# Projecting the second heads' forget gate and queries ahead of the second output gate in layer 1

## The reference

```python
h = rmsnorm(x, pre_norm[layer])
proj = h @ w_in[layer]
(hq, hf, hi, hz, nq, kc, vc, ks, vs, kw, vw, ng, nz) = split(proj)
o_h = hgrn2_mixer(heads(hq), heads(hf), heads(hi), lower_bounds[layer])
o_h = rmsnorm(o_h, hgrn_out_norm[layer]) * silu(hz)
o_n = nsa_mixer(heads(nq), kc, vc, ks, vs, kw, vw, ng, ...) * silu(nz)
x = x + rmsnorm(concatenate([o_h, o_n]) @ w_out[layer], post_norm[layer])
```

## Time and profile before

| | before |
|---|---|
| median of 3 runs | 2059.6 us (2058.7 to 2061.26) |
| profiled execution, its own time | 2056.29 us |
| its span, first to last instruction | 2054.5 us |
| busy TensorE / VectorE / ScalarE / POOL | 2022.3 / 1406.0 / 1061.5 / 105.8 us |
| mean granted clock of TensorE | 0.996 of 2.4 GHz |
| chain that ended last | TensorE 79%, VectorE 4%, ScalarE 2% of the span |

### The profile page before, as it was taken

One profiled execution on the slowest core, in us unless ns is written; L12 is line 12 of the kernel. 1 busy time (PEld: TensorE's weight loads), 2 busy tenths in 40 slices (PEclk: granted clock), 3 DMA queues, 4 the chain that ended last, 5 costly groups with the idle time before them and its releaser, 6 DMA issues.

```text
span 2054.5 us, 30481 instructions
## 1 busy us (share of the span) xinstructions
PE 2022.3 (98%) x12911; PEld 1726.1 (84%) x12911; DVE 1406.0 (68%) x1813; ACT 1061.5 (52%) x1557; POOL 105.8 (5%) x121
## 2 busy tenths in 40 slices
PE   8999999998899999999999999999999999999998
PEld 7889779887778888888898888888888888988887
DVE  6777867778877767647865765766676567656655
ACT  6555646456545544546354545555445554544543
POOL 0100111000210100000000000000100000000000
PEclk9999999999999999999999999999999999999999
DMA  7653345643346754455454465655544554554652
GB/s 268 181 189 124 114 168 173 207 145 103 109 159 221 242 192 147 158 170 164 170 199 164 164 205 188 211 193 196 203 165 144 166 182 165 185 185 144 198 197 87
DMA packets 191090, 356.67 MB, mean 174 GB/s; under 512 B 6317, under 2 KB 83305, under 8 KB 190954
## 3 DMA queue, kind: packets, MB, share of 16 engines
q1 hardware_dynamic: 188218, 344.76, 50.6%
q0 software_dynamic: 2736, 9.96, 1.3%
HBM read 353.65 MB, written 1.05 MB: 173 GB/s over the span
## 4 chain that ended last, share of the span: by engine, by line
PE 79%; DVE 4%; ACT 2%; issue 1%; POOL 0%; DVEq 0%; ACTq 0%
PE bank L2146 15%; PE bank L2150 15%; PE bank L2156 15%; PE bank L2188 13%; PE bank L2192 7%; PE bank L2201 2%; PE bank L2170 2%; PE bank L2173 2%; PE bank L2176 1%; DVE raw_r L2714 1%; PE bank L2222 1%; PE bank L2463 1%; PE bank L2230 1%; PE bank L2241 1%; PE bank L2411 1%
## 5 line engine op out<-in xcount | busy, mean ns | idle before, releaser
L2714 DVE TENSOR_TENSOR raw_r<-raw,high 128x2048 fp32r<-128x2048 f32 (+2 forms) x299 | 674.3, 2266 | 85.4 <-ACT high L2490 84.2
L2490 ACT ACTIVATE high<-raw 128x2048 fp32r<-128x2048 f32 (+2 forms) x299 | 564.6, 1896 | 207.7 <-PE bank L2156 174.7
L2146 PE MATMUL bank<-high,units_r 128*128 128x512 f32 (+3 forms) x1504 | 592.0, 395 | 2.6 <-ACT high L2490 2.1
L2150 PE MATMUL bank<-high,units_r 128*128 128x512 f32 (+2 forms) x1472 | 567.3, 387 | 0.5 <-DVE units_r L2735 0.4
L2156 PE MATMUL bank<-raw_r,units_r 128*128 128x512 f32 (+3 forms) x1504 | 397.0, 385 | 0.0
L2146 PEld LDWEIGHTS bank<-high,units_r 128*128 128x128 f32 x1504 | 283.9, 189 | 62.1 <-issue 4.7
L2156 PEld LDWEIGHTS bank<-raw_r,units_r 128*128 128x128 f32 x1504 | 279.7, 188 | 57.0 <-DVE raw_r L2714 0.3
L2150 PEld LDWEIGHTS bank<-high,units_r 128*128 128x128 f32 x1472 | 278.1, 189 | 54.1 <-DVE units_r L2735 1.7
L2188 PE MATMUL bank<-units_r,high 128*128 128x512 f32 x1152 | 288.2, 392 | 0.0
L2188 PEld LDWEIGHTS bank<-units_r,high 128*128 128x128 f32 x1152 | 208.4, 189 | 38.1
L2192 PEld LDWEIGHTS bank<-units_r,raw_r 128*128 128x128 f32 x1152 | 157.2, 190 | 11.2
(11 more groups left out here) (383 smaller groups left out, 2198.7 us busy)
## 6 DMA issues: line engine op xcount, KB each, us to landing
raw<-in_ffn_w_dram SPq DMA_DIRECT2D x132, 1024.0 KB, 5.1
raw<-in_w_in_dram SPq DMA_DIRECT2D x104, 1024.0 KB, 5.1
raw<-in_w_out_dram SPq DMA_DIRECT2D x24, 1024.0 KB, 5.0
raw<-in_cross_wkv_dram SPq DMA_DIRECT2D x16, 1024.0 KB, 5.0
raw<-in_w_branch_dram SPq DMA_DIRECT2D x12, 1024.0 KB, 4.9
raw<-in_cross_wq_dram SPq DMA_DIRECT2D x8, 1024.0 KB, 5.1
raw<-in_cross_wo_dram SPq DMA_DIRECT2D x8, 1024.0 KB, 4.9
raw<-in_w_in_dram SPq DMA_DIRECT2D x4, 832.0 KB, 4.5
```

Source lines behind the costliest of these rows:

```text
L2146: pe.matmul(o, h.high(k0 + k)[:, span], p.hi[k][:, cols], start=start and k == 0, stop=False, skip_group_check=True)
L2150: pe.matmul(o, h.low(k0 + k)[:, span], p.hi[k][:, cols], start=False, stop=False, skip_group_check=True)
L2490: done = act.activation(high, raw, ACT.Copy)
L2714: done = dve.tensor_tensor(low, raw, high.bitcast(F32), ALU.subtract)
```

## The change

```diff
@@ -1453,8 +1453,11 @@
             yield from nz_proj(0)
             yield from hgrn_v(0)
             yield from hgrn_z(0)
+            if l:
+                yield from hgrn_qf(1)
             yield from nz_proj(1)
-            yield from hgrn_qf(1)
+            if l == 0:
+                yield from hgrn_qf(1)
             yield from hgrn_v(1)
             yield from hgrn_z(1)
             plan.give_pairs(h, ("prod", f"{N}.hz1", 1))
```

## The result

| | before | after |
|---|---|---|
| median | 2057.31 us (9 runs, 2055.87 to 2061.26) | 2063.68 us (9 runs, 2063.12 to 2068.15) |
| ratio, 95% interval | | 1.0033 [1.0023, 1.0043] |
| profiled execution / span | 2056.29 / 2054.5 us | 2063.49 / 2061.7 us |
| TensorE idle, 440 to 600 us | 12.1 us | 15.3 us |
| TensorE work lost to the lower clock, there | 3.8 us | 8.1 us |

The change makes the kernel slower by 0.33%, or 6.4 us between the medians.

The account below looks back on a forecast made before the run. TensorE's work plus its waits bound the kernel. New waits of 14.9 plus 3.8 of clock, 18.7 us, against 15.3 removed give +3.4 us: profiled execution 2059.7, median 2063.0 us, range 2056.5 to 2069.5.

Parts of the forecast that it names:

- What bounds the kernel: TensorE, busy 98% of the span; reordering layer 1's second-half projections can change only waits and clock, winning at most 15.3 us.
- The softplus block: ScalarE runs softplus right behind the split, until 473.25 us; TensorE's pv_few then waits 0.9 us for the small keys' copy.
- The first gate: TensorE's first turn_four of s010 waits 5.0 us for VectorE's gates, ready at 482.8 us; one clock fall follows.
- Rival 2: Faster: first gate held only by exponentials, wait 1.6 us, no fall; -1.9, or -6.5 with level 2 on time; chance 0.12.
- 'same': Second heads' step directly behind s010's second-branch turns: TensorE waits 2.5 us for the key's exponential on ScalarE.
- The second gate: Gate of s110: VectorE finishes 15.2 us after the joint scores start, TensorE arrives after 13.5, so it waits 1.7 us.
- Levels 4 and 2: Second heads' late levels, too little TensorE work between: waits of 1.1, 0.1, 2.9 and 0.7, together 4.8 us.
- The clock: Two falls of TensorE's granted clock, behind the first gate and at levels 4 and 2, 1.9 us each, 3.8 in all.
- Rival 1: Slower beyond measurement: third clock fall at 'same', or VectorE 1 us later at the first gate; +5.3 to +6.3; chance 0.41.
- the bound of 0.2%: Two executions can't be told apart within about 0.2%, 4.1 us; chances: faster 0.10, same 0.49, slower 0.41.

Follow-up runs that it names:

- e2: The changed kernel with the second heads' recurrence of layer 1 begun three units of projection work later, so the 'same' step comes later: 2058.68 us, ratio 1.0006.
- e3: The changed kernel with only the forget gate projected ahead of the second output gate and the queries left behind it: 2054.49 us, ratio 0.9985 to before.
- e11: e3 with softplus left in place but VectorE's forget, bounded and decay begun five projection steps later: 2057.22 us, ratio 0.9996 to before.
- e10: The changed kernel with 3 extra matmuls on TensorE, only ahead of the few keys' step (pv_few of s010): 2063.85 us, ratio 1.0030 to before.
- e5: The changed kernel with extra matmuls on TensorE sized to its six waits, 14.6 us in all: 2059.54 us, ratio 1.0009 to before.
- e6: e3 with all arithmetic on the forget gate (softplus, forget, bounded, decay) begun six projection steps later: 2063.35 us, ratio 1.0023 to before.

## Why the prediction was right or wrong

- *What bounds the kernel* held. Instruction counts are the same, and nearly the whole difference lies in one stretch: the last turn behind it (hT10) starts 7.2 us later and the span is 7.2 longer, with 6.7 of it from the stretch and 0.5 from ahead of it.
- *The softplus block, 0.9.* Right: it runs from 463.97 to 473.86 us and the few keys wait 0.90. But "the waits of 1.0 and 1.1 us were followed by full clock" did not carry over: behind this wait of 0.9 the clock fell, in the change and in e2, e3 and e11 alike. That fall cost nothing, as e10 shows.
- *The first gate, 5.0, held by VectorE.* Right: 5.01 once nothing falls ahead of it (e10), 3.64 as it stood. e11 confirms the mechanism and its size against the exponentials alone: 1.5 us. Rival 2 had that difference at 3.4, by letting the turn start where it put the end of the exponentials (479.4), without the 1.6 us of the last gate behind them; with 1.5 in its place it comes out at no change and not at -1.9.
- *'same', 2.5.* Right: 2.75, held by ScalarE's key; 2.8 with the clock kept up (e5: 2.5 of fillers and 0.3 of waiting).
- *The second gate, 1.7.* **Mis-sized by 2.1**: 3.80, and 3.9 with the clock kept up (3.4 of fillers and 0.45). The chain counted a low split at 2.2 us. The one ahead of these gates took 3.3, since the high split that it needs stood on ScalarE behind eight exponentials and the key's. VectorE's timeline, kernel after:

```profile
531.79 3.29 DVE L2717 TENSOR_TENSOR raw_r<-raw,high 128x2048 fp32r<-128x2048 f32 x1
535.00 0.17 DVE L2983 RECIPROCAL stat<-stat 128x4 f32<-128x4 f32 x1
```

  and ScalarE's:

```profile
531.62 1.05 ACT L2671 ACTIVATE units<-units 128x1024 f32<-128x1024 f32 x1
532.57 1.91 ACT L2493 ACTIVATE high<-raw 128x2048 fp32r<-128x2048 f32 x1
```

  That the low split ends 0.6 us behind the high one is in the rows; that it stalled for it is my reading, and it explains 1.1 of the 2.1.
- *Levels 4 and 2, 4.8.* Near: 1.20 + 2.94 = 4.1. The forecast had 1.1 and 2.9 at the two levels; the other 0.8, at the pv_split and the first step of oh0, did not come.
- *The clock, 2 falls x 1.9 = 3.8.* **The other mis-sized term**: five falls of 1.5 to 1.7 us, 8.1. The Trainium skill, "TensorE: Matmul & The Clock Gate", section "HAM oscillation — how this bites in real kernels", has the price paid again at every long-enough wait, and the trace agrees for every wait of 2.4 us or more. But the price of a fall isn't its size. With the clock kept up in both kernels, the change still costs 17.2 - 12.4 = +4.9 us in the ledger, and the falls add 6.2 - 3.5 = +2.7. So of the 4.2 us between the ledger's +7.6 and the forecast's +3.4, 1.6 belong to waits, hidden in the count of idle time because falls ate into them, and 2.6 to the clock. By the stretch's own length it is 4.0 (1.1 + 2.9) for waits and 2.7 (5.6 - 2.9) for clock, so that the forecast was 0.7 short on waits and 2.6 short on the clock: either way the clock is the larger slip. The times of whole executions don't settle the clock's share: the ratios 1.0033 and 1.0009 put the falls of the change at 4.9 us, 1 and 0.9979 those of before at 4.3, each with an interval of 2 to 3 us to either side. That a fall costs time, in either kernel, they do settle.
- *Rival 1* (a third fall, at 'same') is what happened, and more: its 2065 to 2066 is above the median after, but against before it gave +5.3 to +6.3 and +6.4 was measured. The outcome crossed the bound of 0.2% upward, where I had put 0.41, while the forecast had called no measurable change the likeliest.
- *What the forecast didn't name.* It priced the waits of the new order one by one and never asked which of them come from moving z1 back. e3 shows that to be, together with the early 'same', the whole loss.

## What to carry to other kernels

Move ahead only what heads a long chain (the forget gate, whose softplus to key takes some 30 us over two engines), and leave behind it what is merely needed at the chain's end (the queries): one alone took 3.6 us off, both together added 6.4. Where waits let the clock fall, count the falls one by one, but charge only those whose slowed work ends in no wait that another engine closes; a group of dummy matmuls in the wait shows in one run what a fall costs, and, sized a little under the wait, is itself a small gain. And when a block is moved away from a wait, price the instructions at the place where it arrives.

## What the runs showed of the hardware

- **Length alone didn't decide a fall.** In the profiles of before, the change, e2, e3, e6, e10 and e11, between 440 and 600 us, every wait of TensorE from 2.4 to 8.1 us was followed by a low stretch. Of those from 1.1 to 1.9 us only one was (1.76 us, e2, 551 to 555). The 0.9 us in front of the few keys was followed by one in all four kernels that had it, and those of 0.95 and 1.07 us before by none. With 0.7 of the 0.9 us filled it didn't come.
- **A fall mostly lasted 4 us and cost 1.5 to 1.7**, but four were longer: 2.1 us of loss over 493 to 500 in the kernel before, 3.0 over 507.5 to 514.5 in e11, and in e6 2.2 over 490.5 to 501.5 and 3.1 over 552 to 559.5. In all four the clock had already fallen while TensorE still waited.
- **The table loads drained nothing**: 463.97 + 1.28 = 465.25, with the first softplus instruction at 465.27 us in the change, and in e6 the load at 493.93 ends at 495.21 with the copy behind it at 495.23. The term of the prediction that went by the rows held (0.90 measured), and the 2.8 us that the drain of 1.38 us a load in the Trainium skill ("ScalarE: Activation LUTs", section "What ACT_TABLE_LOAD costs") would have added did not come.
- **A dummy matmul of 128 x 128 in float32 took 0.228 us** (10.0 us for 44), twice what I had sized the first fillers by.
